# Feed-forward activations turned by VectorE in 32x32 blocks instead of by TensorE

## The reference, cut to what matters

```
def _swiglu(h, w_gu, w_down):                      # w_gu 2048 x 11264, w_down 5632 x 2048
    gate, up = jnp.split(h @ w_gu, 2, axis=-1)
    return (jax.nn.silu(gate) * up) @ w_down

x = x + 0.5 * _swiglu(_rmsnorm(x, ffn1_norm), ffn1_w_gu, ffn1_w_down)
x = x + _token_mixing(_rmsnorm(x, mix_norm), ...)
x = x + 0.5 * _swiglu(_rmsnorm(x, ffn2_norm), ffn2_w_gu, ffn2_w_down)

c_act = jax.nn.silu(c)                             # 1 x 2048
for l in range(2):
    mod = c_act @ w_ada[l] + b_ada[l]              # w_ada 2048 x 6144
    shift, scale, gate = jnp.split(mod, 3, axis=-1)
    h = _rmsnorm_2(x, norm_g[l]) * (1.0 + scale) + shift
    ...
```

## Time and profile before

| | us |
|---|---|
| three runs | 3110.33, 3106.94, 3113.41 (median 3110.33) |
| profiled execution | 3100.37, its span 3098.2 |
| granted clock | 0.997 of full speed |
| busy in the span: TensorE, VectorE, ScalarE, GpSimd | 3061.4, 2008.1, 1447.5, 1274.0 |
| moved by DMA | 662.74 MB, mean 214 GB/s |

### The profile page before, as it was taken

One profiled execution on the slowest core, in us unless ns is written; L12 is line 12 of the kernel. 1 busy time (PEld: TensorE's weight loads), 2 busy tenths in 40 slices (PEclk: granted clock), 3 DMA queues, 4 the chain that ended last, 5 costly groups with the idle time before them and its releaser, 6 DMA issues.

```text
span 3098.2 us, 46475 instructions
## 1 busy us (share of the span) xinstructions
PE 3061.4 (99%) x18990; PEld 2702.4 (87%) x18990; DVE 2008.1 (65%) x2494; ACT 1447.5 (47%) x1877; POOL 1274.0 (41%) x621
## 2 busy tenths in 40 slices
PE   8999999999999999999999999999999999999998
PEld 7888888888999999998888888888899998899986
DVE  5778577784323446777567766667469864589764
ACT  6444444344567555544544434444444454544444
POOL 4444444444566554594444444444610004510013
PEclk9999999999999999999999999999999999999999
DMA  7878778785776555465787878787566545565554
GB/s 239 275 246 278 265 260 273 248 287 178 217 180 182 155 166 150 144 176 198 238 269 255 275 248 282 241 287 253 189 193 189 159 143 197 166 189 179 153 167 167
DMA packets 486653, 662.74 MB, mean 214 GB/s; under 512 B 67992, under 2 KB 273544, under 8 KB 486184
## 3 DMA queue, kind: packets, MB, share of 16 engines
q1 hardware_dynamic: 480952, 655.05, 66.2%
q0 software_dynamic: 4448, 2.94, 0.3%
q10 hardware_dynamic: 1040, 1.78, 0.2%
HBM read 655.47 MB, written 2.10 MB: 212 GB/s over the span
## 4 chain that ended last, share of the span: by engine, by line
PE 95%; DVE 2%; ACT 1%; DMA 1%; issue 1%; POOL 0%; ACTq 0%; SPq 0%; DVEq 0%
PE ps L910 34%; PE ps L838 23%; PE ps L915 17%; PE ps L844 11%; PE ps L828 2%; PE ps L869 1%; PE ps L1364 1%; PE ps L1154 1%; PE ps L1135 1%; DVE h_plain L1798 0%; DVE narrow_split_slabs L1853 0%; PE ps L969 0%; PE ps L1062 0%; PE ps L1162 0%; PE ps L1192 0%
## 5 line engine op out<-in xcount | busy, mean ns | idle before, releaser
L789 POOL TENSOR_TENSOR split_slabs<-stage,split_slabs 128x1024 fp32r<-128x1024 f32 x296 | 753.0, 2544 | 1359.9 <-ACT split_slabs L1419 1359.9
L1419 ACT ACTIVATE split_slabs<-stage 128x1024 fp32r<-128x1024 f32 x592 | 627.1, 1061 | 898.3 <-PE ps L915 652.6
L910 PE MATMUL ps<-split_slabs,h_split 128*128 128x512 f32 x3312 | 827.2, 392 | 0.9 <-ACT split_slabs L1419 0.9
L1419 ACT ACTIVATE narrow_split_slabs<-stage 128x1024 fp32r<-128x1024 f32 (+1 forms) x440 | 460.1, 1051 | 637.8 <-PE ps L844 561.0
L838 PE MATMUL ps<-h_split,narrow_split_slabs 128*128 128x256 f32 x5856 | 745.9, 280 | 0.0
L910 PEld LDWEIGHTS ps<-split_slabs,h_split 128*128 128x128 f32 x3312 | 621.0, 188 | 133.4 <-issue 5.1
L838 PEld LDWEIGHTS ps<-h_split,narrow_split_slabs 128*128 128x128 f32 x5856 | 700.5, 188 | 15.7 <-issue 12.3
L1853 DVE TENSOR_TENSOR split_slabs<-stage,split_slabs 128x1024 fp32r<-128x1024 f32 x296 | 404.6, 1369 | 348.3 <-ACT split_slabs L1419 348.0
L789 POOL TENSOR_TENSOR narrow_split_slabs<-stage,narrow_split_slabs 128x1024 fp32r<-128x1024 f32 (+1 forms) x181 | 436.6, 2421 | 311.5 <-ACT narrow_split_slabs L1419 304.0
L915 PE MATMUL ps<-split_slabs,h_split 128*128 128x512 f32 x1656 | 443.0, 389 | 0.3 <-POOL split_slabs L789 0.3
L1853 DVE TENSOR_TENSOR narrow_split_slabs<-stage,narrow_split_slabs 128x1024 fp32r<-128x1024 f32 x259 | 334.8, 1295 | 153.7 <-ACT narrow_split_slabs L1419 152.2
(11 more groups left out here) (253 smaller groups left out, 2163.4 us busy)
## 6 DMA issues: line engine op xcount, KB each, us to landing
stage<-in_w_in SPq DMA_DIRECT2D x360, 512.0 KB, 3.7
stage<-in_ffn_w_gu SPq DMA_DIRECT2D x352, 512.0 KB, 4.9
U<-in_w_ada SPq DMA_DIRECT2D x192, 512.0 KB, 5.6
stage<-in_ffn_w_down SPq DMA_DIRECT2D x176, 512.0 KB, 5.4
stage<-in_w_out SPq DMA_DIRECT2D x96, 512.0 KB, 4.2
stage<-in_w_in SPq DMA_DIRECT2D x80, 128.0 KB, 2.8
stage<-in_w_branch_c SPq DMA_DIRECT2D x32, 192.0 KB, 3.3
stage<-in_cmp_w SPq DMA_DIRECT2D x8, 512.0 KB, 5.5
```

The lines of the kernel that those rows point to most:

```text
L789: nc.gpsimd.tensor_tensor(slab_part(n, 1, size(n)), stage[:, n % RING, 0:size(n)], slab_part(n, 0, size(n)).bitcast(F32), ALU.subtract).th ...
L910: mm(ps[:, 2 * pair + T, :], stationary(kk, i)[:, T * P:(T + 1) * P], w[0][:, kk, :], start=first and kk == 0 and i == 0, stop=False)
L1419: return fn(slab_part(n, 0, size(n)), stage[:, n % RING, 0:size(n)], ACT.Copy)
```

## The change

TensorE's `turn_act` and its calls are taken out. VectorE gets a function of that name that turns the same product with 16 transposes of 32 partitions, four at each of blocks 4, 5, 6 and 7, into the same PSUM banks. ScalarE's rounding moves from block 6 to 10 and VectorE's rest from block 7 to 11. `ADA_AT` is made in another way: 64 blocks in the gate and up slabs, outside positions 3 to 8 of each group, and 32 in the down projection. Slab 16j+5 (j from 1 to 11) leaves `by_vector` in both stages, so GpSimd writes its low part.

```
-ADA_AT = [18 + m * 230 // ADA_LOADS for m in range(ADA_LOADS)]
+ADA_EARLY = 64
+def ada_places():
+    free = [i for i in range(25, GU_SLABS) if i % 16 not in range(3, 9)]
+    early = [free[m * len(free) // ADA_EARLY] for m in range(ADA_EARLY)]
+    late = ADA_LOADS - ADA_EARLY
+    return early + [GU_SLABS + 9 + m * (DOWN * DOWN_GROUPS - 20) // late for m in range(late)]
+ADA_AT = ada_places()
...
+        by_vector -= {s + 16 * j + 5 for s in (S_F1, S_F2) for j in range(1, GU_GROUPS + 1)}
...
-            def turn_act(f, j):
-                at = GU_GROUPS * f + j
-                pe.wait_ge(evacuated, (G_F1, G_F2)[f] + j + 1)
...
-                for c in range(4):
-                    for T in range(TT):
-                        last = transpose(ps[:, 6 + c // 2, (c % 2) * S + T * P:(c % 2) * S + (T + 1) * P],
-                                         u(SILU, P, TT, WN)[:, T, c * P:(c + 1) * P])
-                last.then_inc(act_turned, 1)
...
-                            if side == 0 and q == 2 and j > 0:
-                                turn_act(f, j - 1)
...
-                        if j > 0 and q == 6:
+                        if j > 0 and q == 10:
                             round_act(f, j - 1)
...
+                def turn_act(j, a):
+                    rows = slice(a * SQUARE, (a + 1) * SQUARE)
+                    src = u(SILU, P, TT, WN).rearrange("p t (c w) -> p t c w", c=4)
+                    dst = ps[:, 6:8, :].rearrange("p k (c t s) -> p t (k c) s", c=2, t=TT)
+                    if a == 0:
+                        dve.wait_ge(evacuated, g0 + j + 1)
+                    for b in range(P // SQUARE):
+                        turned_rows = slice(b * SQUARE, (b + 1) * SQUARE)
+                        last = v.transpose(dst[turned_rows, :, :, rows], src[rows, :, :, turned_rows])
+                    if a == P // SQUARE - 1:
+                        last.then_inc(act_turned, 1)
...
                         between(16 * j + q)
-                        if j > 0 and q == 7:
+                        if j > 0 and 4 <= q < 8:
+                            turn_act(j - 1, q - 4)
+                        if j > 0 and q == 11:
                             rest_act(j - 1)
```

More of the change, by code:

```diff
@@ L1027, in ffn @@
                             wide_passes(PAIR[g1 + d], n, act_, q == 0, q == DOWN - 1)
-                        if d == 0 and q == 2:
-                            turn_act(f, GU_GROUPS - 1)
                         between(n - s0)
@@ L1520, in ffn_act @@
                     round_upto(s0 + GU_SLABS + i)
-                    if i == 6:
+                    if i == 10:
                         round_act(f, GU_GROUPS - 1)
@@ L1951, in ffn_vec @@
                     between(GU_SLABS + i)
-                    if i == 7:
+                    if 4 <= i < 8:
+                        turn_act(GU_GROUPS - 1, i - 4)
+                    if i == 11:
                         rest_act(GU_GROUPS - 1)
```

## The result

The changed kernel takes 3125.48 us (median of four runs, 3122.78 to 3129.46) against 3109.47: ratio 1.0059, 95% interval 1.0047 to 1.0072. It is slower by 0.6%. I had forecast 3100 and a range up to 3119. The profiled execution took 3124.9 us, its span is 3123.1, 24.9 longer than before.

The account below looks back on a forecast made before the run. TensorE, busy 3061.4 of 3098.2 us, was taken as the bound. Removing its transposes and a wait gave -20.6 us, late low parts +9.5, so -11 from 3110.33: 3099, rounded up to 3100, range 3087 to 3119.

Parts of the forecast that it names:

- The 69 us: Saving from removing TensorE's transposes if each took the Trainium skill's 390 ns; set aside for the trace's 0.91 us per eight.
- the five named: Slabs 45, 51, 67, 83 and 163 of each feed-forward stage, where VectorE's low part was expected late behind picks.
- the walk to slab 45: Count of VectorE's work from the pick at slab 43: low part of 45 ready at T+8.4, wanted at T+7.25, 1.2 us late.
- What does one cost? ... I take their mean, 0.73: Price of one late low part, from two waits in the earlier trace, 0.46 and 0.99 us; ends 0 and 3.4.
- 13 places: Late low parts expected: 5 in each feed-forward stage plus 3 in the first down projection, +9.5 us together.
- 5.6 us of work in 5.44: Two dense slabs need 5.6 us of the resource VectorE and GpSimd share, against 5.44 of TensorE; priced at no cost.
- SyncE's queue in a rival: Rival of gain given back whole, 3109 us, chance 0.20: 1.5 us a place, including weight loads queued behind block loads.
- 3.6 late: Lateness in us of slab 45's low part if GpSimd, ready for slab 48, takes the shared resource first.
- The slower rival: GpSimd gets the shared resource before the low part at 10 places, 3.4 us each, net +13: 3124 us, chance 0.16.
- 97, 116, 140 and 176 come out in time: Claim that the low parts behind the picks at these four slabs are not late, so they add no cost.
- all stays: Rival that no low part comes later than today and the whole 20.6 us gain remains: 3090 us, chance 0.28.
- the gain is given back: Sign in TensorE's waits for VectorE's low parts: near 20 us if given back, about 1 if kept, 5 to 15 forecast.

Follow-up runs that it names:

- e6: The changed kernel with each pick at block +5 instead of +2 and the running sum in its own tile: 3088.92 us, 0.9941.
- e12: The kernel before with the new block places, the pick at +5 and the sum's own tile, transposes kept on TensorE: 3104.22 us, 1.0000.
- e3: The changed kernel with the low part of slab 16j+5 back on VectorE: 3124.80 us, 1.0058.
- e11: The changed kernel with the pick at +5, the sum's own tile, and the low part of slab 16j+5 back on VectorE: 3088.59 us, 0.9949.
- e4: The changed kernel loading only 2 of 96 adaptive-norm blocks in each stage, with all of VectorE's work kept: 3132.33 us, 1.0082.
- e10: The changed kernel with the pick at block +5 only; the wait before the next sum's first block stays: 3111.39 us, 1.0021.
- e9: The kernel before with nothing but the pick at block +5 and the sum's own tile: 3106.99 us, 1.0004.
- e5: The changed kernel with blocks in the old places and all odd low parts on VectorE, so only the turns move: 3116.42 us, 1.0030.
- e1: The changed kernel with the adaptive-norm blocks back in their old slabs: 3108.05 us, 1.0006.
- e8: The changed kernel with blocks in the old places, the pick at +5 and the sum's own tile: 3107.72 us, 0.9996.

## Why the prediction was wrong, point by point

**Right.** TensorE is the bound and a group's turn costs it about 0.91 us: the stages of e6 are 10.4 us shorter each, and e6 against e12 gives 15 to 18 us for both. The 69 us, an estimate that the prediction gave and put aside, are not seen. The turns into PSUM: 457 ns median, 468 at most, never held by GpSimd, near the lower bound. Silu did not wait for them. The moved low part costs nothing measurable in the new places (e3, e11). The kind of place, blocks and low parts behind a pick, with slabs 45, 51, 67 and 163 of the five named (83 was on time), and the walk to slab 45, which came true to 0.2 us.

**The step that failed: "What does one cost? ... I take their mean, 0.73".** It is the mis-sized term of the sum: 13 places at 0.73, +9.5 us, measured at some 42 us over both stages (28 and 14), about 1.2 us a slab at some 35 slabs. The runs show four things that this price, or the count of 13 places, did not have.

*It was priced as if each place stood alone.* The two rows are from stretches where the blocks lay further apart (one in 2.4 slabs), so that no second race followed. In the dense stretches one did. VectorE's blocks behind the pick delay the next block's load, and the weight loads behind it in SyncE's queue; the slabs then come in a bunch, GpSimd's low parts with them, and each operation of VectorE that meets one takes about 2 us longer. By the traces 1.1 us at slab 45 is followed by 8.7 at slab 51. I had the count of the shared resource, 5.6 us of work in 5.44, and set it to no cost by dividing it over a lead that the pick takes away. I also had SyncE's queue in a rival and gave it no term in the sum; e4 shows that this queue alone isn't the price, since without it slab 45 costs 4.06. That is the prediction's own other branch, "3.6 late" if GpSimd takes the resource first. The slower rival came nearest with 3124 us, but by luck: it had GpSimd winning a single race at ten places, and in the changed kernel GpSimd could not even enter it at slab 45, its slab being late. It missed that one lost race makes the next.

*A wait was missing.* "97, 116, 140 and 176 come out in time" holds for 116 and 176. It fails for 97 (slabs 99 and 100, 7.0 us) and for 140 (slab 141); slab 159, behind the pick at 158, was not on the list either. Where the last block of a sum and the first of the next stand in adjacent slabs (138 and 139, 156 and 157), VectorE stands before that first block, since the sum shares its tile with the low half that TensorE reads. The changed kernel's timeline at slab 141 has this wait of 7.66 us, then block, rest, pick and low part in a row:

```profile
424.70 0.63 DVE L1856 TENSOR_SCALAR U<-U,cact 128x512 f32<-128x512 f32 x1 [7.66 <-PE ps L980]
...
427.35 0.70 DVE L1873 TENSOR_TENSOR ps<-ps,base_consts 128x512 f32<-128x512 f32 x1
...
428.69 1.21 DVE L1846 TENSOR_TENSOR split_slabs<-stage,split_slabs 128x1024 fp32r<-128x1024 f32 x1
...
429.96 1.21 PE L926 MATMUL ps<-split_slabs,h_split 128*128 128x512 f32 x4 [0.79 <-DVE split_slabs L1846]
```

The wait stood in the code (in `ada`, under `k == 0`) and the prediction doesn't name it. In the changed kernel it comes 4 times, 25.1 us of VectorE's standing against 85.2 at the picks, and the slabs behind it (141 to 146, 159) make up about 8 of the 42 us. It is worth more once the picks are late: e10 keeps it, and gets only 14 of the 37 us that e6 gains on the changed kernel.

*The clock.* Behind the three longest stalls of the changed kernel's feed-forward stages TensorE ran at the lower of its levels. The slab after each was late too, 0.8 us at 52, 1.4 at 100, and 1.2 at 52 of the second stage, and the stalled slab lost 0.7 to 1.1 us more than its wait: about 6 us in all. In the earlier trace rows the waits were under 1 us and the clock stayed, so no price taken from there holds this.

*Operations left out.* The small operations of the decay constants, on VectorE at position 1 of groups 2 to 6 of the first stage, were not counted. The timeline at slab 99 shows two of them held for 2.39 and 2.32 us, that at slab 51 one for 2.40. Slabs 51, 52, 99 and 100 cost 16.5 us in the first stage and 4.9 in the second, which has no such operations. That is most of the difference between 28 and 14; no run takes these operations out, so how much of it is theirs is not shown.

**The row I leaned on.** The second of the earlier trace rows, VectorE 41.99 us busy and TensorE never idle, was the ground for "all stays" and for a price near the lowest. e6 shows the same (40.54 busy, no stall). In the changed kernel VectorE is less busy in that window, and TensorE has work for only 36.45 us of it:

```profile
144.40:188.70 44.30, 36.45 (x151) 29.04 (x150) 36.50 (x43) 18.04 (x19) 19.68 (x8) 0.92 0.73 252
```

It was a good row for the amount of work and a wrong one for its order: busy time doesn't say how far the engine is ahead when a wait ends.

**Signs it named.** TensorE's waits for low parts were to be near 20 us if the gain is given back; they were 24.0, and more than the gain went. Of its signs of a wrong mechanism one appeared, but small: TensorE waited 3.0 us for high parts against 0.9 before.

## What to carry to other kernels

An engine that prepares another's work, in order, has a lead over it. A wait for that other engine's latest work uses the lead up, as each pick did here, though the engine was idle while it waited. Before work is added to it, list every wait for the served engine and what stands behind each, also the waits that only guard a shared tile, and move them back until they find their event already there. Here that was three slabs and one tile, and it turned +0.6% into -0.6% with the same work on every engine. In the kernel before, the same move gained nothing (e9): there the waits cost nothing, with less work behind them.

## What the runs showed of the hardware

TensorE's granted clock fell to its lower level (0.50 to 0.53 in windows that lie within it) during or within about 1 us after waits of 1.85, 4.45 and 7.53 us (the changed kernel, at 1639, 310 and 168 us), 2.65 us (e5, at 1599) and 2.91 us (e1, at 360), and stayed there for 3 to 7 us. It stayed at 1.00 through waits of 1.46 us (the changed kernel, at 482), 2.90 us (e8, at 1815) and 2.91 us (e9, at 656). So waits of the same length went both ways, and where the clock fell, the stall's price was more than its own length.

VectorE's operations on 128x32 elements, 0.18 to 0.19 us long, took 2.32 to 2.40 us in three cases in the changed kernel when a GpSimd operation was under way, while a 32x32-block transpose from SBUF into PSUM (436 to 468 ns, 352 times) never did. The section "Who interferes with whom" of the Trainium skill's page SBUF — State Buffer states that a VectorE instruction with two SBUF inputs contends with a GpSimd one that reads SBUF, that `tensor_scalar` can do so through a two-port mode, and that one with at most one SBUF input outside these modes does not. The trace agrees for the transposes and for lines 2003 and 2006, which have two inputs. Line 2001, a `tensor_scalar` with one, was held too (2.40 us); in which mode it ran no run shows.
